# Transposes of the softmax probabilities, their copies and the PV products one slot later in the mixer

## What is computed

```python
for i in range(S // Q_BLOCK):                      # Q_BLOCK = 128, so 4 blocks per head
    q0 = i * Q_BLOCK
    kend = q0 + Q_BLOCK
    s = jnp.einsum('bqhd,bkhd->bhqk', qf[:, q0:kend], kf[:, :kend]) * scale
    bias = c[:, :, q0:kend, None] - c[:, :, None, :kend]
    mask = (q0 + jnp.arange(Q_BLOCK))[:, None] >= jnp.arange(kend)[None, :]
    s = jnp.where(mask, s + bias, -jnp.inf)
    p = jax.nn.softmax(s, axis=-1)
    outs.append(jnp.einsum('bhqk,bkhd->bqhd', p.astype(v.dtype), v[:, :kend]))
```

## Time and profile before

| | us |
|---|---|
| median of 3 runs (lowest, highest) | 1130.69 (1130.41, 1133.49) |
| profiled execution | 1130.75 |
| its span | 1129.0 |
| PE busy in the span | 1099.9 (97%) |
| DVE, ACT busy | 577.5 (51%), 455.7 (40%) |

### The profile page before, as it was taken

How to read it: one execution, slowest core, us unless ns; L and a number is a source line. 1 busy time by engine, 2 the same in 40 slices (tenths; PEclk the granted TensorE clock), 3 DMA queues, 4 the chain that set the end, 5 groups by cost and what they waited for, 6 DMA issues and landing times.

```text
span 1129.0 us, 14939 instructions
## 1 busy us (share of the span) xinstructions
PE 1099.9 (97%) x5910; PEld 948.8 (84%) x5910; DVE 577.5 (51%) x703; ACT 455.7 (40%) x661; POOL 55.2 (5%) x83
## 2 busy tenths in 40 slices
PE   7999999999999999997989999999999999999998
PEld 5888888888888978886777888888899999998886
DVE  5534434353334663554455333437698878763334
ACT  6322222232233573565556222335354455542222
POOL 2000000000001100000000000003700000000001
PEclk9999999999999999998999999999999999999999
DMA  9533332322322444232013435233522423334211
GB/s 300 163 95 93 93 110 87 100 94 97 107 79 56 167 119 126 75 75 57 19 35 94 116 93 167 93 94 105 194 94 75 150 75 116 109 110 152 94 55 75
DMA packets 133331, 118.81 MB, mean 105 GB/s; under 512 B 6416, under 2 KB 119072, under 8 KB 133280
## 3 DMA queue, kind: packets, MB, share of 16 engines
q1 hardware_dynamic: 131104, 113.38, 32.9%
q10 hardware_dynamic: 1456, 2.10, 0.9%
q0 software_dynamic: 720, 2.62, 0.6%
HBM read 109.70 MB, written 6.29 MB: 103 GB/s over the span
## 4 chain that ended last, share of the span: by engine, by line
PE 88%; DVE 5%; ACT 4%; issue 2%; DMA 1%; POOL 0%; SPq 0%; ACTq 0%; DVEq 0%; POOLq 0%
PE bank L1405 24%; PE bank L1395 12%; PE bank L1396 12%; PE bank L1397 12%; PE bank L1525 5%; PE bank L1524 5%; PE bank L1523 5%; PE bank L1637 1%; PE bank L1638 1%; PE bank L1639 1%; PE bank L1460 1%; PE bank L1461 1%; PE bank L1462 1%; DVE w_lo L917 1%; PE bank L1733 1%
## 5 line engine op out<-in xcount | busy, mean ns | idle before, releaser
L917 DVE TENSOR_TENSOR w_lo<-raw,w_hi 128x1024 fp32r<-128x1024 f32 x130 | 166.1, 1279 | 214.6 <-ACT w_hi L503 214.5
L1395 PE MATMUL bank<-u_hi,w_hi 128*128 128x512 f32 x600 | 237.6, 396 | 8.9 <-DVE arena L1278 6.4
L1397 PE MATMUL bank<-u_hi,w_lo 128*128 128x512 f32 x600 | 235.0, 392 | 0.0
L1396 PE MATMUL bank<-u_lo,w_hi 128*128 128x512 f32 x600 | 234.8, 391 | 0.0
L503 ACT ACTIVATE w_hi<-raw 128x1024 fp32r<-128x1024 f32 x130 | 137.1, 1055 | 186.5 <-PE bank L1405 86.2
L1395 PEld LDWEIGHTS bank<-u_hi,w_hi 128*128 128x128 f32 x600 | 113.4, 189 | 32.4 <-issue 9.8
L1397 PEld LDWEIGHTS bank<-u_hi,w_lo 128*128 128x128 f32 x600 | 113.3, 189 | 24.0
L1396 PEld LDWEIGHTS bank<-u_lo,w_hi 128*128 128x128 f32 x600 | 113.5, 189 | 22.4 <-issue 0.2
L1405 PE MATMUL bank<-w_hi,a_hi 128*128 128x512 f32 x408 | 126.0, 390 | 0.0
L1405 PE MATMUL bank<-w_lo,a_hi 128*128 128x512 f32 x408 | 125.7, 389 | 0.0
L1405 PE MATMUL bank<-w_hi,a_lo 128*128 128x512 f32 x408 | 125.7, 389 | 0.0
(11 more groups left out here) (240 smaller groups left out, 1644.6 us busy)
## 6 DMA issues: line engine op xcount, KB each, us to landing
raw<-in_ffn_w_down SPq DMA_DIRECT2D x40, 512.0 KB, 3.4
raw<-in_w_in SPq DMA_DIRECT2D x40, 512.0 KB, 3.8
raw<-in_ffn_w_up SPq DMA_DIRECT2D x26, 512.0 KB, 3.8
raw<-in_ffn_w_gate SPq DMA_DIRECT2D x25, 512.0 KB, 3.8
raw<-in_ffn_w_gate SPq DMA_DIRECT2D x5, 1024.0 KB, 5.4
raw<-in_ffn_w_up SPq DMA_DIRECT2D x5, 1024.0 KB, 7.9
h_store<-h SPq DMA_DIRECT2D x2, 2048.0 KB, 9.7
h<-h_store SPq DMA_DIRECT2D x2, 2048.0 KB, 9.4
```

The costliest lines, as they stand in the source:

```text
L917: V.tensor_tensor(w_lo[:, slot(u), :], raw[:, slot(u), :], w_hi[:, slot(u), :].bitcast(F32), ALU.subtract).then_inc(lo_ready, 1)
L1395: mm(dst, w_hi[:, slot(u), w], rhs_hi[:, k - k0, :], start=k == k0, stop=False)
L1396: mm(dst, w_hi[:, slot(u), w], rhs_lo[:, k - k0, :], start=False, stop=False)
L1397: last = mm(dst, w_lo[:, slot(u), w], rhs_hi[:, k - k0, :], start=False, stop=k == k1)
```

## The change

The three parts that belong together, PE's transposes, ACT's copy and DVE's rest, move from slot s + 2 to slot s + 3. PV of head hh moves from slot 4 hh + 7 to 4 hh + 8, half sum and pair sum from 4 hh + 8 to 4 hh + 9, of_hi and of_lo from 13, 21, ... to 14, 22, .... The loop gets one slot more (39). Scores, fills, scaling, the gated branch and all waits on semaphores keep their slots and counts. The three engines are changed alike; PE's part of the diff, and of the others the lines that give the slots:

```diff
-        SLOTS_B = NS + 6
+        SLOTS_B = NS + 7
...
-                if 2 <= sl < NS + 2:
-                    s = sl - 2
+                if 3 <= sl < NS + 3:
+                    s = sl - 3
                     act.wait_ge(pt_ready, s + 1)
...
-                if sl >= 8 and sl % TT == 0:
-                    hh = sl // TT - 2
+                if sl >= 9 and (sl - 9) % TT == 0:
+                    hh = (sl - 9) // TT
                     act.wait_ge(pv_done, hh + 1)
...
-                if sl >= 13 and (sl - 13) % 8 == 0:
-                    p = (sl - 13) // 8
+                if sl >= 14 and (sl - 14) % 8 == 0:
+                    p = (sl - 14) // 8
                     act.wait_ge(pair_ready, 2 * p + 2)
...
-                if 2 <= sl < NS + 2:
-                    s = sl - 2
+                if 3 <= sl < NS + 3:
+                    s = sl - 3
                     pe.wait_ge(probs_ready, s + 1)
                     if s >= 2:
                         pe.wait_ge(pt_lo, s - 1)
...
-                if sl >= 7 and (sl - 7) % TT == 0:
-                    hh = (sl - 7) // TT
+                if sl >= 8 and sl % TT == 0:
+                    hh = sl // TT - 2
                     pe.wait_ge(pt_lo, TT * hh + TT)
```

## The result

The changed kernel takes 1146.32 us (median of 5 runs, 1144.20 to 1148.07), against 1130.69 (1129.24 to 1133.49) of the kernel before, whose runs beside the experiments below had medians of 1130.6 to 1130.8. The ratio is 1.0137, 95% interval 1.0114 to 1.0160: slower by 1.4%, in the direction forecast and inside the range, 4 us above the number. The profiled execution took 1144.2 us with a span of 1142.5, the fastest of the five. Its span is 13.5 us longer than that of the earlier trace rows.

The account below looks back on a forecast made before the run. PE was taken to hold the kernel up, through its idle time in slots 14 to 36 and its clock. 1130.75 + 8.3 (parts 1 and 2) + 3.4 (clock) = 1142.4 us, range 1134.5 to 1148.

Parts of the forecast that it names:

- The rival in which this gains 8.5 us: Slots 15 to 17: removed waits avert the clock falls from 516 and 530, giving 1122.2 us; chance 0.06.
- Part 1, PV out of its cover: In slots 20, 24, 28, 32 PV follows the fill its gate releases, no longer hidden in idle: 1.31 us each.
- The rival in which ACT and DVE start the chains and PV stays covered: Chains to W24 and W28: PE's 1.31 us vanish in ACT's waits, leaving 1 to 3 us, 1132 to 1134; chance 0.10.
- Part 2, the change of partners: Chains between gates meet other tile sizes and sums: 4 tiles for 1 cost up to 0.73 us, of_hi 0.52.
- W20: PE's 2.53 us wait before slot 20's fill, for DVE's q rest (L1213); term +0.5 us, bounds -1 to +2.
- The tail: After the slots: last pair's half sum and of_hi come behind two Ln/Exp passes on ACT; +0.1 us.
- Part 3, the clock,: PE's granted clock: one short half-clock spell behind each of W24 and W28, 2 x 1.7 = 3.4 us.
- W24: PE's 1.35 us wait before slot 24's fill, for DVE's L1278; term +2.25 us, wait growing to 3.6.
- W28: PE's 2.10 us wait before slot 28's fill, for DVE's L1278; term +2.4 us, wait growing to about 4.5.
- the rival without a further fall: Behind W24 and W28 the clock does not fall again: 1130.75 + 8.3 = 1139.0 us; chance 0.25.
- W32: PE's 2.49 us wait before slot 32's fill, for DVE's L1278; term +1.55 us.
- the rival with long ones: Long half-clock spells behind W24 and W28, as from 530, 10.2 us together: 1149.2 us; chance 0.09.

Follow-up runs that it names:

- The third experiment: The changed kernel with PV moved ahead of the fill inside the same slot, no other edit: 1136.35 us, ratio to before 1.0040.
- the half of the change with PV: Changed kernel with transposes, copies and rests back in slot s + 2, so PV, half sum, pair sum, of_hi alone later: 1143.52 us; 1129.37 with useless matmuls in gaps.
- the best one: Kernel before with ACT's copy or tanh ahead of the exponential in slots 19, 23, 27, 31, plus useless matmuls in PE's gaps: 1119.13 us, ratio 0.9901.

## Why the prediction was right, point by point

**The waits for L813** were taken away, and almost nothing was won by it. Against their 1.7 us stand 1.1 more at L844, where 3.16 us of idle became 4.27 (4.3 forecast), and 0.74 of the new wait for L789, which the prediction did not have. L1695 starts 70.90 us behind the start of the slots and not 71.30: 0.4 us earlier, where 0.5 was forecast. The rival in which this gains 8.5 us is out.

**Part 1, PV out of its cover.** Right. The third experiment shows it by itself: put ahead of the gate's wait in the same slot, PV fills idle time again, which falls by 1.29, 1.28 and 1.23 us before three gates against the changed kernel, and the gates come closer together by about as much (1.27 and 1.16 us, with a spell of 1.7 us in either kernel). The rival in which ACT and DVE start the chains and PV stays covered is out: then the gates would have stood still in that experiment. The 1.31 us of four PVs make 5.2 us; the half of the change with PV cost 5.8 by medians with the bursts, with of_hi and pair sum in it, where 6.8 was expected (5.3 to 7.0 by distance).

**Part 2, the change of partners.** Right to 0.2 us at four of five gates, at full clock (table above). W20 was +0.9 and not +0.5, inside its bounds: the stretch from L1695 to W20 grew by 1.3 us (12.50 to 13.79) and not by 1.0. The table compares one execution of each kernel; the medians differ by 9.0 us where the whole sum was 8.3. of_hi was shown by itself (0.52 us at each of two gates for a term of 0.52). For the transposes alone 2 us were forecast; by distance they cost 2.3, and the 3.1 of the medians has runs in it in which the clock fell. The wait of PV for DVE's rest in slot 15 was not counted, but it moved little: L1695 starts 71.67 us behind the start of the slots there, against 71.31 in the kernel before, both with the clock kept. In the changed kernel that wait does not exist, since PV moved along. The tail cost 0.3 us and not 0.1 (the wait for og, 0.3 to 0.6 us).

**Part 3, the clock,** is the term that was mis-sized. I had priced it at 3.4 us, two short spells behind W24 and W28. Both came, so the rival without a further fall is out, and both were short (1.7 us each). But the clock also worsened where it had already fallen: the spell behind W20 grew from 5.1 to 6.8 us, that behind W32 from 1.7 to 3.4. The rows lack 15.0 us and not the 8.5 + 3.4 = 11.9 of the sum. By distances, the start of the slots to W36 is 13.4 us longer (167.49 against 154.05), of which 8.3 are left with the clock kept, so 5.2 us are the clock in the profiled execution, where 3.4 were forecast. That 1130.75 + 8.3 + 5.2 is again the time of the profiled execution follows from how the two were taken and tests nothing. The step that failed is that I took the three old spells as unchanged.

What makes a spell longer stays open. The gaps in front of the two that grew had grown too (W20 from 2.5 to 4.6, W32 from 2.5 to 4.0), but so had that before L844 (3.16 to 4.27), and its spell stayed at 1.7 us. With of_hi one more slot later the gaps before W20 and W28 were as in the changed kernel (4.63 and 4.35 us, against 4.64 and 4.35), and the losses behind them were 1.7 and 6.8 us where the changed kernel has 6.8 and 1.7. So it was partly luck that both new spells came out short: the rival with long ones did not come, but no run shows that it could not.

The five runs of the changed kernel lie 3.9 us apart, and the slower ones have the lower mean granted clock: 1144.2 us at 0.985, 1146.3 at 0.984, 1148.07 at 0.982. By medians the clock costs 13.7 us in the changed kernel and 7.0 in the kernel before, 6.7 more (twice the 3.4 of the sum), and the rest of the change 9.0 (8.3 in the sum): these two differences are the 4 us by which the median lies above the forecast. Which run gets how many spells was not settled.

The Trainium skill ("TensorE: Matmul & The Clock Gate", section "HAM oscillation — how this bites in real kernels") says that the price of half clock is paid anew after each recurring gap. The five spells behind the five larger gaps of the changed kernel agree, and so does the full clock when the same gaps are shortened by bursts. The gaps of 2.10 and 1.35 us in the kernel before had no spell behind them, and on how much a spell costs here only the rows tell.

## What to carry to other kernels

An instruction that stands in an engine's row right ahead of a wait may be free, and the same instruction right behind it costs its full time where that engine starts the chain to its next wait; so before moving work by a slot, look which waits it passes, not only which of its own inputs are late. To find a bound inside a ring of three engines, follow one gate back until an engine is reached that had nothing to wait for; what that engine does since the gate before adds up, and everything else is slack. And count a gap of TensorE with the spell of half clock that may follow it: the reordering of one ACT instruction in four slots gave 9.2 us here, of which about half is the clock, since with the clock kept on both sides it gave 4.4. That is also how the Trainium skill tells one to work ("Perfetto Trace Analysis", section "Optimization Strategy": find the gaps, see what blocks, make it start sooner), and the 9.2 us agree.

## What the hardware did that I had not expected

- The length of one gap does not decide alone whether the clock falls. In the kernel before it stayed at 1.00 behind 2.10 us of idle, and with the transposes alone later behind 2.23 us before W32, but in that same execution it fell behind 1.80 us (0.64 in the row from 550) and behind 1.89 us (0.54 in the row from 506):

```profile
506.00:508.00 2.00, 2.00 (x9) 0.54 0.15 44
...
550.00:552.00 2.00, 1.98 (x6) 0.64 0.00 0
```

- Nor does it decide how long the clock stays down. With of_hi one more slot later, the gap of 4.35 us before W28 was followed by the long spell, of which these are the first and the last row; in the changed kernel the same gap was followed by a loss of 1.7 us:

```profile
572.00:574.00 2.00, 0.40 (x1) 0.67 0.00 0
...
586.00:588.00 2.00, 2.00 (x13) 0.92 0.00 0
```

- Matmuls of no use in the gaps, 35 in the whole kernel before, made it 7.0 us faster. Where they held the mean clock at 0.999 or above in every run, the runs also lie closer together: 1122.87 to 1124.82 us for that kernel, 1131.31 to 1133.97 for the changed one (1144.20 to 1148.07 without them) and 1119.11 to 1119.44 for the best one (with 22 of them), against 1127.08 to 1133.69 for the kernel before beside it, where the longer runs again have the lower mean clock (0.990 against 0.995). With the transposes alone later they did not hold it in every run (0.995 to 1.000), and those runs lie 4.7 us apart.
